# Five input-projection units beside the adaLN loads, and the residual gate summed in the last gate group

## The chip, the cores and the metric

The kernel runs on one core of a Trainium2 chip. The metric is the device time of one execution in microseconds (us), as the median of several runs. The core has TensorE (matmul; PE in the profile, with its weight loads as PEld), VectorE (DVE), ScalarE (ACT), GpSimd (POOL) and SyncE (SP), which here issues nearly all DMA transfers; each works through its own queue in order and waits on semaphores.

## What is computed

One layer of an encoder trunk, 256 tokens, width D = 2048, all in float32:

```python
mod = c @ ada_w + ada_b                       # one row of 6 x 2048
sh1, sc1, gt1, sh2, sc2, gt2 = split(mod, 6)
h = rmsnorm(x, norm1_g) * (1 + sc1) + sh1
u = h @ w_in                                  # A 512, B 2x512, C 3x512, D 512, gates 4x2048
y_a = pool_mixer(u_A); y_b = conformer_conv(u_B)   # B: a * sigmoid(gate), conv 31, LayerNorm, silu, @ w
y_c = (bg * conv3(cg * xv)) @ sc_w_out             # C
y_d = fft2(u_D).real @ fnet_w_out                  # D
merged = sum_k sigmoid(gate_k) * y_k
x = x + gt1 * (merged @ w_o)
h2 = rmsnorm(x, norm2_g) * (1 + sc2) + sh2
x = x + gt2 * hier_moe(h2, ...)               # 32 experts, top 1 group of 4, top 2 of 8
return rmsnorm(x, final_g)
```

## The kernel before

The four engine programs are written by hand, each a straight list of instructions with semaphores. `h` is held transposed (`hT`: 16 k tiles of 128 channels x 256 tokens). The ring has 7 slots of 2 MiB (128 x 4096 elements); slots 0 to 3 take weight blocks in turn, slot 4 (`BW`) the branch weights, slot 5 (`ADA`) adaLN tiles, slot 6 later `h_hi`.

**The head.** Shift and scale of the first modulation are vector-matrix products over 2 x 16 MiB of `ada_w`. VectorE makes them: for each k tile it multiplies the weight rows by `c` and adds them to `acc` (L1294, L1296); TensorE then sums over the partitions by products with a column of ones (`head_sums`, L541), VectorE adds the bias (L1304, L1306), and ScalarE modulates four k tiles (L1033). This is done in four parts of 512 columns, so that a quarter of `hT` is ready at a time. With each part TensorE takes the first `HEAD` = 3 of seven input units (512 columns of `w_in` each, `UNIT_COLS`: B gate, B value, C, C, C, D, A) over the four k tiles that are ready (L557), into six of the eight PSUM banks; the last two banks hold the sums. SP's order for a part is four ada blocks of 2 MiB (`load_head`, L350), then three weight blocks of 1 MiB (`load_head_w`, L359).

**The other units.** Units 3 and 4 (the third and first column blocks of C) run after the head over all 16 k tiles (`unit_T`, L571), then units 5 and 6 (`unit_N`, L584), with the two LayerNorm sums between them (L593, L600), then the DFT products (L612, L634, L635) and the pooling (L620). VectorE makes the convolution of 31 taps (L1332 to L1335) and that of 3 (L1353). GT1 (16 MiB of `ada_w`) is loaded in eight blocks (`load_gt1`, L384), summed by VectorE between its other steps (L1276, L1278), reduced by 32 one-column products (L640), and kept as a column.

**The gates.** Four groups of four units of 512 columns, each over 16 k tiles. Every weight is split in two float32r halves: ScalarE copies the high half (`gate_high`, L1095), VectorE subtracts for the low half (`gate_low`, L1403), `AHEAD` = 3 pieces of 128 x 1024 ahead, and TensorE makes three products for each (L658 to L660), eight pieces a unit. Behind each unit stand the branch's own products (`gate_y`, L628), with VectorE's merging (L1451, L1456). Beside groups 0 to 2 the adaLN vectors SH2, SC2 and GT2 are summed from tiles of 1 MiB (L1394) and reduced (`sum_ada`, L690). SP issues for each unit two gate blocks of 2 MiB (L363), behind each two adaLN tiles (L417), and behind every other unit's tiles a 2 MiB block of branch weights (L444). Group 3 has no adaLN tiles. GT1's row is made from its column there: VectorE spreads it on a diagonal (`diag`, L1478), TensorE multiplies by ones (`gate_row`, L709), ScalarE copies (L1121). Then come `w_o`, the router and the experts.

```python
def ada_tiles(g, k, n):
    vec = SH2 + g
    for i in range(n):
        sp.wait_ge(acc_step, ADA1 + 16 * g + k + i - 1)
        sp.dma_start(slot(ADA)[:, i % 2 * D:(i % 2 + 1) * D], ada_v[:, k + i, vec * D:(vec + 1) * D]
                     ).then_inc(ada_tile[i % 2], 16)
```

## Time and profile before

| | us |
|---|---|
| runs, not profiled | 1859.21, 1859.7, 1860.25 |
| median | 1859.7 |
| profiled execution, its own time | 1858.33 |
| its span, first to last instruction | 1856.5 |
| TensorE matmul busy | 1763.9 (95%) |
| VectorE busy | 899.4 (48%) |
| ScalarE busy | 393.7 (21%) |
| DMA | 641.92 MB, mean 346 GB/s |
| mean granted TensorE clock | 0.981 |

All times in the rows are from the start of the span. The slices cut the span in 40 equal parts of 46.4 us; a digit is the busy share in tenths. The chain of work that ended last is followed back from the last instruction, at each step to what released it. A matmul of float32 data is listed as two instructions.

### The profile page before, as it was taken

To read this page: it belongs to the slowest core of one execution; us is meant where nothing else is said; L and a number is where in the kernel's file an instruction comes from. 1 tells how busy PE (TensorE), PEld (TensorE's weight loads), DVE (VectorE), ACT (ScalarE), POOL (GpSimd) and SP (SyncE) were. 2 spreads that over 40 slices of the span, in tenths; PEclk is the share of its full clock that TensorE was granted. 3 is DMA by queue.
4 is the path that set the end of the run, shared out by engine and by line. 5 is a ranking of instruction groups with operands and counts; after the bars stand their busy time and mean duration, and the time that the engine had idled before them with its cause. 6 is when DMAs were issued, how large, how long until landed. Compare 5 with 4: busy or idle time off the path is not lost.

```text
span 1856.5 us, 26120 instructions
## 1 busy us (share of the span) xinstructions
PE 1763.9 (95%) x10306; PEld 1016.1 (55%) x10306; DVE 899.4 (48%) x1087; ACT 393.7 (21%) x477; POOL 0.9 (0%) x5
## 2 busy tenths in 40 slices
PE   1979999999999999999999999999999999999996
PEld 1868747786777677687444444444444443434342
DVE  5876766866757644457432333333233332323334
ACT  3010014432322333334211101111011111101011
POOL 0000000000000000000000000000000000000000
PEclk8989999989989999999999999999999999999998
DMA  9996597779868945355699999999999999999995
GB/s 374 386 387 257 191 378 291 295 274 351 303 249 317 339 151 212 148 189 237 247 422 422 422 422 422 422 422 422 423 421 422 422 422 422 422 423 421 422 422 237
DMA packets 137004, 641.92 MB, mean 346 GB/s; under 512 B 8578, under 2 KB 8706, under 8 KB 76674
## 3 DMA queue, kind: packets, MB, share of 16 engines
q1 hardware_dynamic: 136256, 637.08, 86.2%
q10 hardware_dynamic: 562, 2.55, 0.4%
q0 software_dynamic: 144, 1.70, 0.2%
q8 instruction: 30, 0.49, 0.1%
q14 instruction: 12, 0.10, 0.0%
HBM read 639.20 MB, written 2.10 MB: 345 GB/s over the span
## 4 chain that ended last, share of the span: by engine, by line
PE 68%; DMA 24%; DVE 6%; ACT 1%; issue 1%; SPq 0%; DVEq 0%; ACTq 0%
DMA ring<-in_exp_w 19%; PE ps L925 16%; PE ps L889 6%; PE ps L658 5%; PE ps L659 5%; PE ps L660 5%; PE ps L628 5%; DVE r_m L1296 4%; PE ps L912 3%; PE ps L867 3%; PE ps L571 3%; PE ps L584 3%; DMA ring<-in_branch_w 2%; DMA ring<-in_ada_w 2%; PE ps L753 2%; PE ps L754 2%
## 5 line engine op out<-in xcount | busy, mean ns | idle before, releaser
L925 PE MATMUL ps<-ring 128*64 128x512 f32 x2048 | 464.8, 596 | 5.8 <-DMA ring<-in_exp_w 5.8
L925 PEld LDWEIGHTS ps<-ring 128*64 128x64 f32 x2048 | 143.1, 137 | 291.7 <-issue 291.7
L1664 DVE TENSOR_TENSOR r_h<-r_h,ps 128x1024 f32<-128x1024 f32 x124 | 145.8, 1218 | 205.8 <-PE ps L912 205.8
L659 PE MATMUL ps<-g_lo,h_hi 128*128 128x512 f32 x512 | 201.7, 394 | 0.0
L1637 DVE TENSOR_TENSOR r_c<-ps,scale 128x512 f32<-128x512 f32 x65 | 44.7, 688 | 292.6 <-PE ps L867 291.7
L1209 ACT ACTIVATE r_m<-ps 128x512 f32<-128x512 f32 x32 | 19.1, 597 | 697.7 <-PE ps L925 697.7
L658 PE MATMUL ps<-mix_hi,h_hi 128*128 128x512 f32 x384 | 157.9, 411 | 0.0
L1095 ACT ACTIVATE mix_hi<-ring 128x1024 fp32r<-128x1024 f32 x96 | 101.7, 1062 | 261.1 <-PE ps L660 261.1
L1403 DVE TENSOR_TENSOR g_lo<-ring,mix_hi 128x1024 fp32r<-128x1024 f32 x96 | 117.5, 1225 | 77.7 <-ACT mix_hi L1095 76.9
L660 PE MATMUL ps<-mix_hi,h_lo 128*128 128x512 f32 x384 | 151.6, 395 | 0.0
L867 PEld LDWEIGHTS ps<-r_c,xparts 128*128 128x128 bf16 x3120 | 108.8, 118 | 50.9 <-issue 49.5
L912 PE MATMUL ps<-ring,r_m 64*128 64x512 f32 x496 | 123.2, 615 | 0.0
L867 PE MATMUL ps<-r_c,xparts 128*128 128x64 bf16 x3120 | 115.8, 198 | 1.3 <-ACT xparts L1164 1.3
L889 PE MATMUL ps<-r_b,r_c 128*64 128x512 f32 x496 | 113.3, 598 | 0.0
L889 PE MATMUL ps<-ring,r_c 128*64 128x512 f32 x496 | 111.7, 592 | 0.0
L659 PEld LDWEIGHTS ps<-g_lo,h_hi 128*128 128x128 f32 x512 | 97.7, 191 | 23.2 <-issue 3.1
L1394 DVE SCALAR_TENSOR_TENSOR r_m<-ring,col,r_m 128x2048 f32<-128x2048 f32 x45 | 105.5, 2345 | 0.0
L628 PE MATMUL ps<-ring,r_b 128*128 128x512 f32 x208 | 94.2, 604 | 10.3 <-DMA ring<-in_branch_w 6.0
L557 PE MATMUL ps<-r_h,ring 128*128 128x256 f32 x384 | 90.8, 401 | 5.0 <-ACT r_h L1033 5.0
L1296 DVE SCALAR_TENSOR_TENSOR r_m<-ring,col,r_m 128x512 f32<-128x512 f32 x120 | 90.2, 752 | 4.3
L557 PEld LDWEIGHTS ps<-r_h,ring 128*128 128x128 f32 x384 | 77.7, 203 | 16.9 <-issue 5.3
L912 PEld LDWEIGHTS ps<-ring,r_m 64*128 64x128 f32 x496 | 42.7, 186 | 79.5 <-issue 79.5
(267 smaller groups left out, 1745.8 us busy)
## 6 DMA issues: line engine op xcount, KB each, us to landing
ring<-in_exp_w SPq DMA_DIRECT2D x320, 1024.0 KB, 20.2
ring<-in_w_in SPq DMA_DIRECT2D x40, 2048.0 KB, 10.1
r_b<-in_exp_w SPq DMA_DIRECT2D x64, 1024.0 KB, 22.1
ring<-in_ada_w SPq DMA_DIRECT2D x24, 2048.0 KB, 18.7
ring<-in_ada_w SPq DMA_DIRECT2D x48, 1024.0 KB, 5.1
ring<-in_w_o SPq DMA_DIRECT2D x8, 2048.0 KB, 7.7
ring<-in_w_in SPq DMA_DIRECT2D x12, 1024.0 KB, 14.9
ring<-in_branch_w SPq DMA_DIRECT2D x6, 2048.0 KB, 9.7
```

Source lines behind the costliest of these rows:

```text
L557: last = mm(u[:, f, :], head_w(i)[:, kk, f * P:(f + 1) * P], hT[:, k, :], start=(k == 0 and f % 2 == 0), stop=(k == KT - 1), skip_group_ch ...
L628: last = mm(ps[:, y_bank(n) + t, :], lhs(k, t), rhs(k), start=(k == 0), stop=(k == kts - 1))
L658: mm(ps[:, b + t, :], h, hi[:, cols], start=(k == 0), stop=False)
L659: mm(ps[:, b + t, :], h, lo[:, cols], start=False, stop=False)
L660: last = mm(ps[:, b + t, :], h_lo[:, k, t * P:(t + 1) * P], hi[:, cols], start=False, stop=(k == KT - 1))
L867: last = mm(gat[:, kk, :], xparts_k[:, i, t, k // 4, k % 4, :], chosen[:, t, 0:NWIN], start=(t == 0 and i == 0), stop=(t == TT - 1 and i = ...
L889: last = mm(ps[side * NWIN:(side + 1) * NWIN, 4 + b, :], hid[:, f, :], chunk(CHUNKS + f)[:, q * MIX:(q + 1) * MIX], start=(f == 0), stop=( ...
L912: last = mm(ps[:, (6, 4)[b] + side, :], pair_wT[half, t * P:(t + 1) * P], y_sb[half, b, :], start=True, stop=True)
L925: last = mm(ps[m * NWIN:(m + 1) * NWIN, 2, :], xe[:, k, :], chunk(2 * c + m)[:, kk * F:(kk + 1) * F], start=(k == 0), stop=(k == KT - 1))
L1296: ins = V.scalar_tensor_tensor(out=total, in0=w, scalar=ccol[:, k:k + 1], in1=total, op0=ALU.mult, op1=ALU.add)
L1403: V.tensor_tensor(g_lo[:, q, (x % 4) * 1024:(x % 4 + 1) * 1024], slot(q)[:, (x % 4) * 1024:(x % 4 + 1) * 1024], g_hi[x % 4].bitcast(F32), ...
L1664: V.tensor_tensor(x1n, x1n, ps[:, (6, 4)[b]:(6, 4)[b] + 2, :].rearrange("p b n -> p (b n)"), ALU.add).then_inc(added, 1)
```

## The change

- The head carries five units. `HEAD` is 5; units 3 and 4 are made in each part over its four k tiles, one after the other into the same two banks that also hold the sums, and VectorE adds each quarter to a total in SBUF (`add_part`, `late`). `ORDER` is the order of the units in a part. `unit_T` is gone.
- The ada blocks hold four k tiles of both vectors, VectorE's step is 1024 elements wide and there are 64 of them rather than 128. Three blocks instead of four are in flight (slots 5, 6 and the room of `r_b`), the weights use slots 0 to 4.
- x is loaded by SP ahead of everything else, no longer by ScalarE's queue; `mix_consts` waits for the third part.
- GT1 leaves the middle. It is loaded in the last gate group in 32 half tiles of 512 KB (`gt1_tile`), issued by SP behind the group's gate blocks, and summed by VectorE behind each `gate_low` (`gt1_piece`) onto an accumulator that was zeroed and has the bias in its first partition. TensorE makes the row straight from it with a product of ones; `diag` and its column are gone. Two blocks of `w_o` are issued between the tiles.
- Unit 5 and half of unit 6 run ahead of the first LayerNorm sum. The root, the last LayerNorm product and Silu are moved behind the first three gate pieces; `h_hi` is made earlier.

The core of the diff (SP, then TensorE, ScalarE, VectorE):

```diff
-ADA_FIRST = 4
-HEAD = 3
+ADA_FIRST = 3
+HEAD = 5
+ORDER = [[3, 0, 4, 1, 2]] * 3 + [[3, 0, 1, 4, 2]]
...
+        def head_ada(i):
+            return (slot(5), slot(6), r_b[:, :])[i % ADA_FIRST].rearrange("p (k v n) -> p k v n", k=4, v=2)
+
+        def used(part, n):
+            return HEAD * part + ORDER[part].index(n) + 1
...
+            def load_head(part, piece):
+                i = 4 * part + piece
                 if i >= ADA_FIRST:
-                    sp.wait_ge(acc_step, 8 * (i - ADA_FIRST + 1))
...
+                    sp.wait_ge(acc_step, 4 * (i - ADA_FIRST + 1))
+                elif i == 2:
+                    sp.wait_ge(sq_done, 2)
+                for v in range(2):
+                    sp.dma_start(head_ada(i)[:, :, v, :],
+                                 ada_v[:, 4 * piece:4 * piece + 4, v * D + part * PART:v * D + (part + 1) * PART]
+                                 ).then_inc(ada_in[i % ADA_FIRST], 16)
...
-                if q == 3:
-                    sp.wait_ge(acc_step, 104)
-                elif q < 7:
-                    sp.wait_ge(head_used, (8, 10, 12)[q - 4])
-                else:
-                    sp.wait_ge(w_used, q - 6)
+                sp.wait_ge(head_used, (3 * HEAD, 3 * HEAD, used(3, 0), used(3, 2))[q - Q_UNIT])
...
+            sp.dma_start(x_in, x_v).then_inc(x_loaded, 16)
...
+            def gt1_tile(k, half):
+                if k:
+                    sp.wait_ge(acc_step, ADA2 + 2 * (k - 1) + half + 1)
+                else:
+                    sp.wait_ge(acc_step, ADA2)
+                sp.dma_start(slot(ADA)[:, 2048 + half * 1024:3072 + half * 1024],
+                             ada_v[:, k, GT1 * D + half * 1024:GT1 * D + (half + 1) * 1024]).then_inc(ada_tile[half], 16)
...
                         if g < N_BRANCH - 1:
                             ada_tiles(g, 4 * j + 2 * i, 2)
+                        else:
+                            if j == 0 and i == 0:
+                                sp.wait_ge(acc_zero, 1)
+                                sp.dma_start(acc[0:1, :], gt1_bias).then_inc(bias_in, 16)
+                            if j == 3:
+                                load_wo(i)
+                            for k in (4 * j + 2 * i, 4 * j + 2 * i + 1):
+                                for half in range(2):
+                                    gt1_tile(k, half)
...
+            pool.wait_ge(head_used, 3 * HEAD)
             pool.dma_start(r_c[:, :], mix_consts).then_inc(mixc_in, 16)
...
+                pe.wait_ge(acc_step, 16 * (part + 1))
+                if part:
+                    pe.wait_ge(part_added, 2 * part)
...
-                for n in range(HEAD):
+                for n in ORDER[part]:
...
+                    if n == 4:
+                        pe.wait_ge(part_added, 2 * part + 1)
+                    u = tiles((0, 4, 2, 6, 6)[n])
...
-                        if n == 0:
+                        if n == 3:
                             pe.wait_ge(h_ready, k + 1)
...
+            pe.wait_ge(sig_ready, 1)
+            unit_N(5, (0, 1))
+            pe.wait_ge(v_ready, 1)
+            unit_N(6, (0,))
             pe.wait_ge(conv_done, 1)
+            pe.wait_ge(part_added, 8)
...
+            unit_N(6, (1,))
...
-            pe.wait_ge(acc_step, ADA1)
-            for k in range(KT):
-                last = mm(ps[:, 6, k:k + 1], acc[:, k * P:(k + 1) * P], ones[:, 0:1], start=True, stop=True)
-            last.then_inc(summed, 1)
...
-                    last = mm(ps[:, 4 + m, :], ones, diag[:, o:o + 4, :], start=True, stop=True)
+                    n = 2 * half + m
+                    last = mm(ps[:, 4 + n, :], ones, acc[:, n * MIX:(n + 1) * MIX], start=True, stop=True)
...
-            pe.wait_ge(row_saved, 1)
+            pe.wait_ge(acc_step, ADA2 + 32)
+            pe.wait_ge(unit_saved, UNITS - 1)
+            gate_row(0)
+            pe.wait_ge(m_parts, 3)
             gate_row(1)
...
             for x in range(AHEAD):
                 gate_high(0, x)
+            act.wait_ge(inv_ready, 2)
+            A(mean, mean, ACT.Sqrt).then_inc(root_done, 1)
+            act.wait_ge(conv_done, 3)
+            for m in range(MT):
+                A(brT[:, 1, m, :], brT[:, 1, m, :], ACT.Silu, bias=col[:, C_LNB + m:C_LNB + m + 1],
+                  scale=col[:, C_LNG + m:C_LNG + m + 1]).then_inc(conf_ready, 1)
...
+            def add_part(part, n):
+                v.wait_ge(head_used, used(part, n))
+                total = late[:, n - 3, :]
+                products = ps[:, 6:8, :].rearrange("p b n -> p (b n)")
+                if part == 0:
+                    ins = V.tensor_copy(total, products)
+                else:
+                    ins = V.tensor_tensor(total, total, products, ALU.add)
+                ins.then_inc(part_added, 1)
+                v.wait_ge(part_added, 2 * part + n - 2)
+
+            for part in range(4):
+                total = head_acc(part)
+                for k in range(KT):
+                    i = 4 * part + k // 4
+                    if part and k in (0, 8):
+                        add_part(part - 1, 3 + k // 8)
+                    if k % 4 == 0:
+                        v.wait_ge(ada_in[i % ADA_FIRST], 32 * (i // ADA_FIRST + 1))
+                    w = head_ada(i)[:, k % 4, :, :]
...
+            add_part(3, 3)
+            v.wait_ge(head_used, used(3, 1))
+            v.wait_ge(sig_ready, 1)
...
+            v.wait_ge(root_done, 2)
+            V.tensor_tensor(brT[:, 1, :, :], brT[:, 1, :, :], mean.unsqueeze(1).broadcast_to([P, MT, S]),
+                            ALU.mult).then_inc(conv_done, 1)
...
+            def gt1_piece(k, half):
+                v.wait_ge(ada_tile[half], 3 * 128 + 16 * (k + 1))
+                v.wait_ge(bias_in, 16)
+                cols = acc[:, half * 1024:(half + 1) * 1024]
+                V.scalar_tensor_tensor(out=cols, in0=slot(ADA)[:, 2048 + half * 1024:3072 + half * 1024],
+                                       scalar=ccol[:, k:k + 1], in1=cols, op0=ALU.mult, op1=ALU.add
+                                       ).then_inc(acc_step, 1)
...
-                        if not last and i % 2 == 1:
+                        if last:
+                            gt1_piece(4 * j + i // 2, i % 2)
+                        elif i % 2 == 1:
                             ada_one(g, 4 * j + i // 2)
...
-            v.wait_ge(mod_ready, 8)
-            V.tensor_tensor(diag, ident.unsqueeze(1).broadcast_to([P, KT, P]),
-                            mod[:, GT1, :].unsqueeze(2).broadcast_to([P, KT, P]), ALU.mult).then_inc(diag_ready, 1)
+            v.wait_ge(mod_ready, 7)
+            V.memset(acc, 0.0).then_inc(acc_zero, 1)
```

## Rows read from the trace of the kernel before

**Rows 1.** Slices of the span: DMA share in tenths, GB/s.

```profile
DMA  9996597779868945355699999999999999999995
GB/s 374 386 387 257 191 378 291 295 274 351 303 249 317 339 151 212 148 189 237 247 422 422 422 422 422 422 422 422 423 421 422 422 422 422 422 423 421 422 422 237
```

**Rows 2.** Stretch: busy (x) per engine; last: TensorE clock, DMA, GB/s.

```profile
60.00:70.00 10.00, 10.00 (x48) 8.81 (x47) 9.54 (x14) 0.00 (x0) 0.00 (x0) 1.00 1.05 387
```

**Rows 3.** Timeline, head: start, us, engine, line, operation, count [idle before].

```profile
46.80 1.86 PE L541 MATMUL ps<-keep,r_m 128*128 128x1 f32 x8 [11.09 <-DVE r_m L1296]
...
49.97 22.85 PE L557 MATMUL ps<-r_h,ring 128*128 128x256 f32 x96 [1.31 <-ACT r_h L1033]
...
72.66 2.11 PE L541 MATMUL ps<-keep,r_m 128*128 128x1 f32 x16
...
76.03 20.96 PE L557 MATMUL ps<-r_h,ring 128*128 128x256 f32 x96 [1.25 <-ACT r_h L1033]
```

**Rows 4.** Groups, 0 to 320 us: xcount | busy us, mean ns | idle.

```profile
L1296 DVE SCALAR_TENSOR_TENSOR r_m<-ring,col,r_m 128x512 f32<-128x512 f32 x120 | 90.2, 752 | 4.3
...
L571 PE MATMUL ps<-r_h,ring 128*128 128x256 f32 x256 | 55.4, 379 | 0.0
...
L1278 DVE SCALAR_TENSOR_TENSOR r_m<-ring,col,r_m 128x2048 f32<-128x2048 f32 x15 | 35.3, 2352 | 15.5 <-DMA ring<-in_ada_w 15.2
...
L1324 DVE TENSOR_TENSOR r_m<-ps,r_m 128x1024 f32<-128x1024 f32 x1 | 1.2, 1228 | 17.8 <-PE ps L557 17.8
```

**Rows 5.** Chain of work that ended last: start us, us, what.

```profile
160.50 55.25 PE ps L571 x256
215.75 1.73 PE ps L593 x8
...
287.91 3.46 PE ps L640 x32
...
317.55 3.78 PE ps L628 x4
...
344.16 1.72 PE ps L628 x4
...
522.06 7.24 PE ps L690 x32
```

**Rows 6.** Timeline, ScalarE and VectorE ahead of the first gate.

```profile
253.80 2.07 ACT L1054 ACTIVATE r_b<-r_b,col 128x256 f32<-128x256 f32 x4
...
288.87 2.94 ACT L1095 ACTIVATE mix_hi<-ring 128x1024 fp32r<-128x1024 f32 x3
...
289.95 3.50 DVE L1403 TENSOR_TENSOR g_lo<-ring,mix_hi 128x1024 fp32r<-128x1024 f32 x3 [5.19 <-ACT mix_hi L1095]
```

**Rows 7.** Stretches around the pool product, columns as in rows 2.

```profile
313.00:317.50 4.50, 0.27 (x2) 0.00 (x0) 4.46 (x2) 1.97 (x2) 0.00 (x0) 0.90 1.03 369
317.50:321.50 4.00, 3.95 (x5) 1.85 (x6) 0.14 (x1) 0.00 (x0) 0.00 (x0) 0.50 0.99 400
```

**Rows 8.** Chain, group 1's second branch matrix.

```profile
473.75 2.27 DVE r_m L1394
...
476.41 9.80 DMA ring<-in_branch_w
486.25 7.13 PE ps L628 x16
```

**Rows 9.** Line 417, the adaLN tiles of 1 MiB: least, median and most.

```profile
DMA to landing us min/median/max: 4.8/5.1/13.8
```

**Rows 10.** DMA issues, 481 to 488 us: xcount, KB, us to landing.

```profile
ring<-in_ada_w SPq DMA_DIRECT2D x2, 1024.0 KB, 11.7
ring<-in_w_in SPq DMA_DIRECT2D x1, 2048.0 KB, 15.6
```

**Rows 11.** Chain around the last gate group's first unit.

```profile
649.65 3.47 PE ps L690 x32
...
675.04 6.87 PE ps L628 x16
```

More of the change, by code:

```diff
@@ L74, in build @@
 def build(nc, x, ada_w, w_in, pool_w, pool_scale, branch_w, w_o, router_w, exp_w1, exp_w3, exp_w2, final_g,
-          columns, router_b, keep_consts, mix_consts, iota_const, out):
+          columns, router_b, gt1_bias, keep_consts, mix_consts, iota_const, out):
     with ExitStack() as ctx:
@@ L204, in build @@
         ada_in = [sem(f"ada_in{i}") for i in range(ADA_FIRST)]
-        ada_more = [sem(f"ada_more{i}") for i in range(2)]
+        part_added = sem("part_added")
+        sig_ready = sem("sig_ready")
+        v_ready = sem("v_ready")
+        cx_ready = sem("cx_ready")
+        acc_zero = sem("acc_zero")
+        bias_in = sem("bias_in")
         ada_tile = [sem(f"ada_tile{i}") for i in range(2)]
@@ L357, in load_head_w @@
                 if part >= 2:
-                    sp.wait_ge(head_used, HEAD * (part - 2) + n + 1)
+                    sp.wait_ge(head_used, used(part - 2, n))
                 sp.dma_start(head_w(i), win_v[:, 4 * part:4 * part + 4, UNIT_COLS[n]:UNIT_COLS[n] + MIX]
@@ L445, in _ @@
                                      br_v[g - 1, :, :, j * MIX:(j + 2) * MIX]).then_inc(bw_in, 16)
-            for n in range(8):
+            for n in range(2, 8):
                 if n == 2:
@@ L547, in _, with unit_N @@
                 head_sums(part)
[L548 removed]
+                for n in ORDER[part]:
                     i = HEAD * (part % 2) + n
                     pe.wait_ge(head_w_in[i], 16 * (part // 2 + 1))
[L551 removed]
+                    if n == 4:
+                        pe.wait_ge(part_added, 2 * part + 1)
+                    u = tiles((0, 4, 2, 6, 6)[n])
                     for kk in range(4):
                         k = 4 * part + kk
[L554 removed]
+                        if n == 3:
                             pe.wait_ge(h_ready, k + 1)
                         for f in range(4):
+                            if n < 3:
+                                begin, end = k == 0, k == KT - 1
+                            else:
+                                begin, end = kk == 0, kk == 3
                             last = mm(u[:, f, :], head_w(i)[:, kk, f * P:(f + 1) * P], hT[:, k, :],
[L558 removed]
+                                      start=(begin and f % 2 == 0), stop=end, skip_group_check=True)
                     last.then_inc(head_used, 1)
[L561 to L577 removed]
+            def unit_N(n, halves):
+                for half in halves:
                     q = Q_UNIT + 2 * (n - HEAD) + half
@@ L1277, in ada_chunk @@
                     else:
[L1278 removed]
+                        ins = V.scalar_tensor_tensor(out=total, in0=w, scalar=ccol[:, k:k + 1], in1=total,
                                                      op0=ALU.mult, op1=ALU.add)
[L1280 to L1299 removed]
@@ L1300, in _ @@
+                    ins.then_inc(acc_step, 1)
+                    v.wait_ge(acc_step, 16 * part + k + 1)
                 ks = slice(4 * part, 4 * part + 4)
@@ L1340, in _ @@
             v.sem_inc(conv_done, 1)
-            v.wait_ge(w_used, 2)
-            v.wait_ge(unit_saved, 3)
-            step(V.tensor_tensor(cxpad[:, :, 1:1 + S], tiles(4), tmp[0].rearrange("p (c t) -> p c t", c=MT), ALU.mult))
-            v.sem_inc(unit_saved, 1)
-            z = tmp[0].rearrange("p (c t) -> p c t", c=MT)
+            add_part(3, 4)
+            v.wait_ge(head_used, used(3, 2))
+            step(V.tensor_tensor(cxpad[:, :, 1:1 + S], tiles(2), late[:, 0, :].rearrange("p (c t) -> p c t", c=MT), ALU.mult))
+            v.sem_inc(cx_ready, 1)
             c0 = steps[0]
@@ L1405, in gate_low @@
                                 ALU.subtract).then_inc(g_lo_done, 1)
-            v.wait_ge(h_split, 1)
-            v.wait_ge(w_used, 8)
-            for i in range(4):
+            v.wait_ge(w_used, 4)
+            for i in range(2, 4):
                 V.tensor_tensor(h_lo[:, 4 * i:4 * i + 4, :], hT[:, 4 * i:4 * i + 4, :],
```

210 lines of the change are left out of this document (58 added, 152 removed).

## The prediction

> **What bounds the kernel now.** I read the slices first, then the stages by stretches, then the chain of work in order of time. Up to some 140 us the transfer engines are full and TensorE is not: the slices show the share and the rate of the transfers, and the stretch shows 387 GB/s and the full TensorE clock side by side [rows 1, 2]. From 160 us on TensorE is busy all the time up to the experts, whose weights fill the transfer engines again from some 915 us to the end, at 422 GB/s [rows 1]. The chain says the same: VectorE's sums beside the loads, then TensorE from 160.50 on, units 3 and 4 in 55.25 us, unit 5, unit 6 and the mixers up to 291 [rows 5]. So whatever makes TensorE reach the experts earlier is worth its full length, and whatever makes it wait in between costs its full length. The change does one of each: it takes two units out of the TensorE-bound stretch and puts them beside the loads (a gain), and it puts 32 transfers of GT1 into the last gate group, ahead of that group's branch weights in SP's queue (a wait). The answer is the difference of the two.
>
> **The five units beside the loads.** A unit of 16 k tiles takes 55.4/2 = 27.7 us at the full clock (256 instructions, 216 ns from one to the next) [rows 4, 5], so a quarter of it takes 6.92 us, and three quarters 20.8 us, which is the 20.96 us measured once TensorE was warm [rows 3]. Five quarters are 34.6 us. Between two parts lie the sums, their read-out and ScalarE's first modulation: 72.8 to 76.03, that is 3.2 us, 3.3 taken [rows 3]. A part then costs TensorE 37.9 us.
> The transfers of a part grow from 11 to 13 MiB, 13.6 MB, 35.2 us at 387 GB/s [rows 2]. VectorE's 16 steps of 1024 elements have no row; 512 elements take 752 ns and 2048 take 2352 [rows 4], so 1.29 us each, 1.32 with the gap, 21.1 us a part, plus two adds of 1.23 us (the row of a product out of PSUM [rows 4]) and small steps: 24.5 us. But its second add waits for the third unit of the part before; from there 1.25 + 8 x 1.32 = 11.8 us are left, against 13.8 us of TensorE's last two units. So TensorE bounds the parts, by 2 us before VectorE and 2.7 before the transfers.
> The first part: x now goes first on SP's queue, then the pieces of 2 MiB at 5.4 us each. From about 2 us on at that rate, x and the small constants end at about 9, the pieces land at 14.9, 20.3, 25.7 and, since the fourth waits for the first to be used up, 31.1; four steps later it is 36.4. Before, the sums were ready at 46.8 and the units began at 49.97, 3.2 us on, with half of the sums done earlier [rows 3]; with both halves behind the last step I take 5.1. The units begin at 41.5. Then 34.6 + 2.2 (the cold start: 22.85 against 20.7 [rows 3]) + 3 x 37.9 gives 192.0 for the end of all five, where the old kernel ends units 3 and 4 at 215.75 [rows 5]. **Term 1: -23.8 us.** From both sides: if the first part starts only when it did, -15; if every gap were free, -34.
> The long convolution starts on VectorE when three units of the last part are there, at 178.2, and takes 50.5 as before: 229. TensorE asks for it only after unit 5 and half of unit 6, at 192 + 41.2 = 233. It stays hidden, with 4 us to spare. mix_consts and the four loads of units 5 and 6 go out from about 154 on and have more than 20 us.
>
> **Between the units and the gates.** Unit 5, unit 6, the two LayerNorm sums, the DFT and pooling are the same instructions. GT1's 32 one-column products (3.46 us [rows 5]) fall away, but the first gate piece still needs ScalarE's copy and VectorE's rest behind the last DFT copy, and these ended at 291.2 in the old kernel, just as the 3.46 us did [rows 5, 6]. So that removal is worth nothing: TensorE waits 3.3 us instead. Moved behind three gate copies are now the root, VectorE's product and four Silu steps, with two table loads, some 5.3 us on ScalarE (2.07 of it the Silu steps [rows 6], the rest the root, the hand-overs and the loads); TensorE has three pieces of 2.73 us in hand then. By my count piece 3 is ready 0.3 us late, and VectorE is 1.4 us behind at the end of the first gate unit, where TensorE already waited 4.3 us, to 317.55, for its product on the pool weights [rows 5, 7]. **Term 2: +1.7 us** (0 to 4).
>
> **The last gate group.** Here the order on SP's queue decides. For each four pieces it issues a 2 MiB gate block and two weight tiles; the 2 MiB of branch weights come after the eighth piece's tiles, for units 0 and 2 of a group. In groups 1 and 2 that is how it is already: the branch weights are issued at 476.41, right after VectorE's step at 473.75 to 476.02 released the last tile, they land 9.8 us later, and TensorE, which was ready at 485.0, starts at 486.25 [rows 8]. In group 3 the old kernel has no tiles, its branch weights go out early and TensorE never waits: 653.1 to 675.04 is the bare 21.9 us of a unit [rows 11].
> Now group 3 has half tiles, (k, half), and the issue of one waits for the step on the same half one k before. The last one ahead of the branch weights, (3,1), waits for the step on (2,1), which VectorE runs behind the rest of piece 5 of the unit. At best that is 5 x 2.73 + 1.07 + 1.24 + 1.32 = 17.3 us into the unit, against 12.8 for group 1. With 0.5 MiB ahead, the branch weights take 9.8 - 1.35 = 8.5 us: 26.5 at best, where TensorE needs them at 21.8 (22.7 in unit 2, after the turning of merged). So 4.7 and 3.8 us of waiting are the floor.
> I don't take the floor, because the half tiles themselves are late. One is issued only two pieces (5.4 us) before it is used. No row has one of 0.5 MiB; 1 MiB takes 4.8 to 5.1 us when nothing is ahead, and up to 13.8 when something is [rows 9], so 3.5 (estimate: 1.35 less) to 4.8. But before k = 2 and 3 (and 10 and 11) SP has put a gate block of 2 MiB, and the queue is served in order: a 1 MiB tile issued behind 2 MiB blocks took 11.7, and a block 15.6 [rows 10]. So (2,0), issued at 12.9, lands at 20.9 instead of 16.4. Stepping through unit 0 from TensorE's first gate product: the memset and its hand-over 2.0, the bias row and (0,0) land by 6.3, steps end at 7.6, 10.2, 12.9, 15.4, then the block holds up (2,0): 22.2, 24.8; branch weights issued at 25.6, landed at 34. TensorE needs them at 21.8: it waits 12.3 us. Unit 2 in the same way: it waits 8.9 us. At the 422 GB/s of the experts' slices [rows 1] it is 11.1 and 7.9. The middle of the two sums: **Term 3: +20.1 us** (8.5 to 23). The pieces in between stay ahead of TensorE, and GT1's last step ends 2 us before the last branch product does. The four products of the row take the same time as before, and the last copy of it is as exposed as it was.
>
> **The clock.** After 4.3 us of idling the granted clock fell to 0.50, and 4 products took 3.78 us instead of 1.72, the next unit 1 us more: 3.1 us in all [rows 5, 7]. Both waits of group 3 are longer than that. **Term 4: +6.3 us.** The shorter gaps are open. Of 3.2 us, filled half with one-column products, one passed at full clock (72.8 to 76.0 [rows 3]); such products alone, in sum_ada, once came with half the clock (7.24 us for 3.46 us of them [rows 5]) and once did not (3.47 [rows 11]). There are four such chances now, three between parts and the one ahead of the gates; I count one stretch of 3.2 us. **Term 5: +3.2 us** (0 to 13). The sums of groups 0 and 1 were both cold in the old kernel, some 6.5 us each with what follows them; that they come out otherwise can give back up to 13 us.
> The Trainium skill ("TensorE: Matmul & The Clock Gate", Part 1: The HAM clock gate) says that the throttled state is the default, and that the monitor runs freely, so that the same products meet it in different phases. That agrees with the two unlike sums above, and it is why I leave the sums' phases as they were and widen the range.
>
> **Sum.** -23.8 + 1.7 + 20.1 + 6.3 + 3.2 = +7.5 us. The profiled execution took 1858.3 us (span 1856.5 and 1.8 around it); that gives 1865.8, and for the median of the runs, 1859.7, 1867.2.
>
> **Rivals.** (1) Faster: the branch weights of group 3 aren't held up by the blocks, VectorE keeps pace, and the waits are the floor, 4.7 + 3.8. The first is then about as long as the one that dropped the clock, the second shorter: +3.1. -23.8 + 1.7 + 8.5 + 3.1 = -10.5, 1849; with one warm sum less, 1852. For it: the tiles are small and 16 engines serve them. Against it: every branch load of groups 1 and 2 took its 9.7 to 11 us in order. It decides from a total wait in group 3 below 12 us. A cold sum that turns warm helps to this side too. 0.2.
> (2) No change: the forecast with the waits right, and one cold sum phase gone (-6.5), 1861. 0.2.
> (3) The parts are longer than TensorE's work: VectorE's second add and the slots of three pieces make the loop. At 2 us of slack, a step of 1.5 us rather than 1.32 adds 1.2 us a part; steps of 1.6 (752 x 2 and the gap, the nearest row doubled) add 2.5 us in each of three parts and 4 in the first: +10, 1878. 0.12.
> (4) Every gap of 3.3 us halves the clock: four stretches instead of one, +9.6, 1877. The page named above speaks for it where it says that idling throttles; the row at 72.8 speaks against. 0.13.
> The forecast itself has 0.35.
>
> **How the numbers follow.** Eight in ten lie between 1850 and 1881: the floor of the waits at one end, rivals 3 and 4 with a little over at the other. A measurement of this kernel tells about 0.2%, 3.7 us, from no change. Faster by more: rival 1, 0.2. Within it: rival 2, 0.2. Slower by more: forecast and rivals 3 and 4, 0.6.
>
> **What would show it.** Term 1: units end near 192, each part 38 us apart, TensorE busy from 41 on. Term 2: the first gate product some 3.3 us after the last DFT product. Term 3: in the last group the branch weights are issued about 25 and 21 us into units 0 and 2, and TensorE waits for them 12 and 9 us, in two pieces. Term 4: a clock of 0.50 behind both. It would be wrong if the branch weights landed within 24 us of the unit's start, or if the head ended above 200 or below 185.

## The result and the profile after

The changed kernel took 1866.57 us (median of 12 runs, 1860.85 to 1874.83) beside 1859.01 us for the kernel before (12 runs, 1857.37 to 1861.1): a ratio of 1.0045, 95% interval 1.0031 to 1.0059. It is slower by 7.6 us, twice the 3.7 us (0.2%) that the prediction took as the least that can be told from no change; the forecast was 1867.2. The profiled execution has a span of 1864.2 us where the old one had 1856.5.

First the chain of work through the head and up to the gates (start us, us, what). L579 is the line of the five head units, L592 units 5 and 6, L1285 VectorE's steps, L636 the products of a branch.

```profile
1.74 13.40 DMA ring<-in_ada_w
...
15.95 1.30 DVE r_m L1285
...
41.74 36.55 PE ps L579 x160
...
81.22 34.77 PE ps L579 x160
...
156.61 36.46 PE ps L579 x160
193.07 41.20 PE ps L592 x96
...
295.14 3.78 PE ps L636 x4
```

Five units end at 193.07, where the old kernel ended units 3 and 4 at 215.75 [rows 5]; VectorE's step takes 1.30 us, and a part repeats every 37.7 us where no clock was lost. The product on the pool weights, L636 at 295.14, answers to 317.55 [rows 5]. TensorE waits twice on the way there, for the first gate piece and just ahead of that product, where the old kernel waited 4.28 us; its timeline (in brackets the idle time before, and what ended it):

```profile
268.54 0.50 PE L661 MATMUL ps<-mix_hi,h_hi 128*128 128x512 f32 x1 [3.32 <-DVE g_lo L1376]
...
295.14 3.78 PE L636 MATMUL ps<-ring,r_b 128*128 128x512 f32 x4 [4.50 <-DVE ring L1400]
```

Then the last gate group, in the same chain, from the reduction of GT2 (L692) to the first product on w_o (L751). Transfers from in_ada_w are GT1's half tiles; L711 is the product of ones that makes GT1's row.

```profile
625.20 3.48 PE ps L692 x32
...
641.99 8.39 DMA ring<-in_ada_w
...
654.53 8.98 DMA ring<-in_branch_w
663.56 8.63 PE ps L636 x16
...
725.48 9.16 DMA ring<-in_branch_w
734.68 8.90 PE ps L636 x16
...
766.25 6.87 PE ps L636 x16
773.12 3.45 PE ps L711 x8
...
777.66 0.50 PE ps L751
```

The branch weights of unit 0 were issued at 654.53, 25.9 us behind the first gate product, and landed at 663.51; in the old kernel the same products followed theirs without a gap [rows 11]. The waits of this stretch, 625 to 780 us (us in all, times, longest):

```profile
DVE r_m L1413 <- DMA ring<-in_ada_w: 24.9, 15, 5.1
...
PE ps L636 <- DMA ring<-in_branch_w: 21.7, 2, 11.4
```

SyncE's timeline shows why they were late: the issue of the branch weights (L462) stands behind four half tiles (L423), and each of those waits for a step of VectorE. An entry that lasts 12 us is the queue standing at such waits; ahead of unit 2's branch weights, issued at 725.48, it stands for 13.35 us.

```profile
641.99 12.51 SPq L423 DMA_DIRECT2D ring<-in_ada_w  x4
654.53 0.43 SPq L462 DMA_DIRECT2D ring<-in_branch_w  x1
```

Of line 423, the half tiles, the time to landing was, answering to rows 9 and 10 of before:

```profile
DMA to landing us min/median/max: 3.6/4.5/13.3
```

And the stretches (columns as in rows 2): after, the whole last group and its two waits; before, the same group.

```profile
629.00:778.00 149.00, 126.23 (x482) 90.40 (x480) 94.21 (x76) 41.45 (x40) 0.00 (x0) 0.92 0.73 267
...
656.00:667.00 11.00, 3.44 (x5) 1.65 (x6) 3.37 (x3) 0.00 (x0) 0.00 (x0) 0.53 1.01 393
728.00:739.00 11.00, 4.32 (x6) 1.90 (x7) 3.53 (x3) 0.00 (x0) 0.00 (x0) 0.53 1.02 415
```

```profile
653.00:775.00 122.00, 120.93 (x482) 88.10 (x481) 54.81 (x45) 41.43 (x40) 0.00 (x0) 1.00 0.46 168
```

The account by places, as starts of the same work:

| | before | after | difference |
|---|---|---|---|
| the head's last unit ends (before: units 3 and 4) | 215.75 | 193.07 | -22.7 |
| product on the pool weights | 317.55 | 295.14 | -22.4 |
| first product of the last group | 653.1 | 628.7 | -24.4 |
| first product on w_o | 775.05 | 777.66 | +2.6 |
| end of the span | 1856.5 | 1864.2 | +7.7 |

Everything that the head gave (24.4 us) went in one group of gates, which grew by 27.0 us. Another 5.1 us came behind it, of which two stretches at half the clock in the w_o stage, 786 to 790 and 861 to 865, are some 3.4 us (1.7 each, the time lost by a clock of 0.57 over 4 us); where the other 1.7 went wasn't looked into.

### The profile page after: what moved, and what is told of

It is laid out like the page before. It is cut to its first block, busy times and chain, and to the rows that moved or that the text cites. A ratio compares the mean times of both kernels' runs of the same rounds, so it can differ in the third digit from the quotient of the medians.

```text
span 1864.2 us, 26124 instructions
## 1 busy us (share of the span) xinstructions
PE 1766.5 (95%) x10273; PEld 1013.6 (54%) x10274; DVE 899.9 (48%) x1046; ACT 392.7 (21%) x476; POOL 0.8 (0%) x5
## 4 chain that ended last, share of the span: by engine, by line
PE 70%; DMA 22%; DVE 4%; ACT 1%; issue 1%; SPq 0%; DVEq 0%; ACTq 0%
PE ps L923 18%; DMA ring<-in_exp_w 15%; PE ps L579 8%; PE ps L887 8%; PE ps L636 5%; DMA ring<-in_ada_w 4%; PE ps L910 4%; PE ps L865 4%; PE ps L661 4%; PE ps L663 4%; PE ps L662 4%; DMA ring<-in_branch_w 3%; PE ps L592 3%; PE ps L751 2%; PE ps L753 2%; PE ps L752 2%
## 5 line engine op out<-in xcount | busy, mean ns | idle before, releaser
L579 PE MATMUL ps<-r_h,ring 128*128 128x256 f32 x640 | 142.6, 386 | 5.0 <-ACT r_h L1030 5.0
L579 PEld LDWEIGHTS ps<-r_h,ring 128*128 128x128 f32 x640 | 123.7, 194 | 22.6 <-issue 5.3
L636 PE MATMUL ps<-ring,r_b 128*128 128x512 f32 x208 | 97.6, 622 | 30.8 <-DMA ring<-in_branch_w 26.3
L661 PEld LDWEIGHTS ps<-mix_hi,h_hi 128*128 128x128 f32 x384 | 74.1, 193 | 21.9 <-DVE g_lo L1376 3.7
## 6 DMA issues: line engine op xcount, KB each, us to landing
ring<-in_exp_w SPq DMA_DIRECT2D x320, 1024.0 KB, 19.7
```

Of the source, the lines that this page charges most:

```text
L579: last = mm(u[:, f, :], head_w(i)[:, kk, f * P:(f + 1) * P], hT[:, k, :], start=(begin and f % 2 == 0), stop=end, skip_group_check=True)
L636: last = mm(ps[:, y_bank(n) + t, :], lhs(k, t), rhs(k), start=(k == 0), stop=(k == kts - 1))
L661: mm(ps[:, b + t, :], h, hi[:, cols], start=(k == 0), stop=False)
```

## The experiments

Each kernel is the changed one with the edit shown. Ratios are to the kernel before, on the same chip.

**The changed kernel again.** 

> The changed kernel as it is, profiled and timed once more, as the measure for the other kernels and for its spread. In the profile shown of it the last gate group took 148.9 us from the end of the third sum (628.7) to the first product with w_o (777.7), against 121.9 before, and TensorE waited 11.4 and 10.3 us in it for branch weights. Queue theory (the waits are made by the order on SP's queue): the same two waits within 0.5 us. Clock theory for the spread of 14 us between its runs: the waits repeat and the stretches with a clock of 0.50 lie elsewhere or are of other length. Rival (transfers differ from run to run): the waits themselves differ by some us. Time 1866, between 1860 and 1874.

1866.66 us (5 runs, 1863.02 to 1871.5) beside 1860.22; ratio 1.0042 (1.0029 to 1.0054). The two waits in its last group are 22.3 us, the longer 11.7: they repeat, with the order of the queue.

**The branch weights ahead of the tiles.**

`branch_w` holds the wait and the transfer of L462.

```diff
+    if j == 0 and i == 0:
+        branch_w(g, 0)
     for k in (4 * j + 2 * i, 4 * j + 2 * i + 1):
         for half in range(2):
             gt1_tile(k, half)
+    if j == 2 and i == 0:
+        branch_w(g, 2)
```

> Only SP's order in the last gate group changes: the branch weights of unit 0 are issued ahead of all half tiles, those of unit 2 behind the first four tiles of that unit. The same transfers, the same VectorE steps. Queue theory: both waits (21.7 us) go, and with them most of the 10.2 us lost to a clock of 0.50 in that group; the group takes 122 to 125 us, the kernel 24 to 27 us less than the changed one, some 1841. Rival (the group is longer because 16 MiB of tiles and 32 VectorE steps load it): the group stays above 140 us, the kernel gains under 8 us, 1859 or more.

1846.96 us (6 runs, 1845.98 to 1851.27), ratio 0.9936 (0.9923 to 0.9948): 19.7 us less than the changed kernel on the same chip, and faster than the kernel before. TensorE no longer waits for branch weights. But the group still takes 135 us, not the 122 to 125 that were expected, nor the 140 and more of the rival, and the kernel lies 6 us above the 1841 that were expected. Its chain now runs through the tiles alone (L1420 is L1413 here, L718 is L711):

```profile
639.83 9.51 DMA ring<-in_ada_w
649.36 1.30 DVE r_m L1420
650.67 3.83 DMA ring<-in_ada_w
...
753.66 1.30 DVE r_m L1420
755.00 5.41 PE ps L718 x8
```

Transfer, step, transfer, step, to the end of the group: each transfer waits for the step that frees its place, and no long wait of TensorE covers this loop any more. A half tile takes some 3.8 us when nothing is ahead and 8.3 to 9.5 when a block of 2 MiB is. VectorE waits 36.0 us for them in this group, so its gate pieces come late, and the row's product (L718) comes 2.9 us late behind VectorE's last step:

```profile
PE ps L668 <- DVE g_lo L1383: 6.0, 3, 3.4
```

So there were two mechanisms in the last group, and the prediction had only the first.

**GT1 taken out.** This kernel leaves out GT1's tiles and VectorE's sum of them; the row is the bias alone.

```diff
-    for k in (4 * j + 2 * i, 4 * j + 2 * i + 1):
-        for half in range(2):
-            gt1_tile(k, half)
...
-    if last:
-        gt1_piece(4 * j + i // 2, i % 2)
```

> Leaves GT1's sum out: no half tiles are loaded and no steps on them are made, the row is the bias alone; the branch weights keep their place in SP's program. It shows what GT1 costs in the last group in any order. Queue theory: as e1 within 3 us, since with a better order GT1 is hidden: group 121 to 123 us, kernel 1839. Rival (tiles and steps load the group by themselves): this kernel is 10 us or more faster than e1.

1833.19 us (4 runs, 1832.26 to 1833.84), ratio 0.9857 (0.9842 to 0.9871). The last group is bare TensorE work: 122.11 us of 123.

```profile
626.00:749.00 123.00, 122.11 (x480) 88.91 (x479) 54.05 (x44) 41.26 (x40) 0.00 (x0) 0.99 0.51 188
```

This is the floor for any way of loading GT1 there. The order of the queue is worth 19.7 us of the distance to it, and 13.8 us were still missing: more than the 3 us expected, and what the rival had asked for (10 us or more). Which of tiles, steps and latency makes them is not told by this run. Also, its runs lay 1.6 us apart, those of the changed kernel 8.5 to 14.

**A gate block out from between the tiles.**

```diff
-    if x < 8 or g < N_BRANCH - 1:
+    if g < N_BRANCH - 1:
         gate_w(g, x)
+    elif i == 0 and x < 8:
+        gate_w(g, x)
+        gate_w(g, x + 1)
```

> In the last group the second 2 MiB gate block of each unit is issued ahead of the unit's first tiles, no longer between tiles of k 1 and k 2 (and 9 and 10). The branch weights stay behind eight half tiles. The forecast split the waits in two: a floor of 4.7 and 3.8 us (the chain of steps that releases the last tile) and the rest from tiles held up behind that block. If that is right: branch weights issued some 21 and 18 us into units 0 and 2, waits of 6 to 8 and 4 to 6 us, sum 10 to 14 instead of 21.7, kernel 8 to 14 us less, 1852 to 1858. Rival (tiles are slow on their own, by their size or by VectorE): the waits stay within 3 us of 21.7 in sum.

1859.24 us (10 runs, 1854.38 to 1862.37), ratio 0.9996 (0.9987 to 1.0005): no difference to the kernel before, 7.4 us less than the changed one. In the chain the branch weights go out 22 us into the unit instead of 26 (L639 is L636 here, L1416 is L1413):

```profile
646.47 1.29 DVE r_m L1416
...
648.15 9.24 DMA ring<-in_branch_w
```

The waits of the group:

```profile
PE ps L639 <- DMA ring<-in_branch_w: 16.0, 2, 8.3
```

The waits fall from 22.3 to 16.0 us, where 10 to 14 had been expected and 19 or more by the rival. A part of them is the held-up tiles, as Term 3 had it; the larger part stays, and in the chain the last tile ahead of the branch weights still waits for a step of VectorE (646.47).

**The tiles on GpSimd's queue.** GT1's bias row goes there too, and the tiles have semaphores of their own.

```diff
 def gt1_tile(k, half):
     if k:
-        sp.wait_ge(acc_step, ADA2 + 2 * (k - 1) + half + 1)
+        pool.wait_ge(acc_step, ADA2 + 2 * (k - 1) + half + 1)
...
-    sp.dma_start(slot(ADA)[:, 2048 + half * 1024:3072 + half * 1024],
+    pool.dma_start(slot(ADA)[:, 2048 + half * 1024:3072 + half * 1024],
```

> The half tiles of GT1 are issued by GpSimd, which is idle, with the same waits; SP's program in the last group is that of the kernel before, with no wait for a tile in it. In e1 the chain of work in that group ran through the tiles alone: a load of 3.7 us or, behind a 2 MiB block, 8.3 to 9.5 us, then a step of 1.30 us, sixteen times over, and the group took 139 us from the end of its sum to the copy of the row. Loop theory (the tile loop is bound by its own latency, and the blocks ahead in the same queue make it too long): with a queue of its own a tile takes some 4 to 5 us throughout, 16 x 6 = 96 us, hidden; branch weights go out early; the group takes 119 to 123 us and the kernel comes within 4 us of e2, 1834 to 1838. Rival (the tiles' bytes or VectorE's 32 steps are the load): the group stays over 130 us, the kernel over 1843.

1854.74 us (12 runs, 1848.96 to 1861.73), ratio 0.9975 (0.9962 to 0.9988), 17 to 21 us above what was expected and within what the rival had asked for (over 1843; the tiles' bytes or VectorE's steps as the load). The run with both edits, below, has the same bytes and steps and none of this loss. TensorE waits for no branch weights here, and yet the group takes 137.7 us: the tiles no longer stand behind the blocks in SP's queue, but they are in flight beside them. The median to landing was 4.8 us by the page of the profile (4.5 for those of SP in the changed kernel), single ones took far longer, and the loop is the same. The chain of work, then the waits of VectorE and TensorE over the group:

```profile
703.68 10.09 DMA ring<-in_ada_w
```

```profile
DVE r_m L1413 <- DMA ring<-in_ada_w: 33.8, 19, 6.0
...
PE ps L661 <- DVE g_lo L1376: 9.6, 3, 4.8
```

Here the second queue took away the order and left the latency. Whether a tile issued by GpSimd is a little slower by itself was not tested.

The Trainium skill ("DMA: Bandwidth & Descriptors", Issuing engines are not separate DMA queues) says that transfers issued by SyncE, ScalarE and GpSimd run on the same 16 DMA engines. The trace agrees as far as it goes: VectorE's wait in this group is 33.8 us with GpSimd's queue and 36.0 with SyncE's (branch weights first in both).

**Four places for the half tiles.** The first half of `r_b` (branches 0 and 1) is not read in the last group; each place has a semaphore of its own.

```diff
+gt1_slot = [r_b[:, 0:2048], ring[:, 5, 2048:4096]]
 def gt1_tile(k, half):
-    if k:
-        sp.wait_ge(acc_step, ADA2 + 2 * (k - 1) + half + 1)
+    if k > 1:
+        sp.wait_ge(acc_step, ADA2 + 2 * (k - 2) + half + 1)
...
-    sp.dma_start(slot(ADA)[:, 2048 + half * 1024:3072 + half * 1024],
+    sp.dma_start(gt1_slot[k % 2][:, half * 1024:(half + 1) * 1024],
```

> The changed kernel, in which GT1's half tiles have four places rather than two: those of even k go to two thirds of the branch tiles' buffer that the last group no longer reads, those of odd k stay where they were. The issue of one then waits for the step two k before, not one. Order on SP's queue unchanged. Theory (the lead of the tiles sets both the tile loop and the late branch weights): the last tile ahead of the first branch weights waits for the step on (1,1), which ends about 12.8 us into the unit, not some 20; branch weights issued some 13 to 15 us in, landed at 22 to 25, waits 0 to 3 us each, 4 in sum (changed kernel 21.7), DVE waits for tiles under 10 us (24.9), the last group 124 to 128 us (148.9), kernel 1842 to 1848. Rival (the gate blocks of 2 MiB in the same queue set the pace, whatever the lead): waits for the branch weights stay above 12, the group above 137, kernel above 1853.

1845.98 us (5 runs, 1842.07 to 1850.53) beside 1859.14; ratio 0.9921 (0.9907 to 0.9935). With the order untouched, the longer lead alone takes away more than the change had cost (chain, then waits of the group; L638 is L636, L1415 is L1413):

```profile
649.55 12.36 DMA ring<-in_branch_w
```

```profile
PE ps L638 <- DMA ring<-in_branch_w: 6.1, 2, 4.8
DVE r_m L1415 <- DMA r_b<-in_ada_w: 5.9, 2, 3.4
```

The branch weights go out 16 us into the unit (633.6 to 649.55; 13 to 15 expected) and take 12.4 us with more in front of them, so the waits are 6.1 us rather than 4, and the group takes 131.6 us rather than 124 to 128. The total is within what was expected (1842 to 1848).

**Both: branch weights first, four places.** The edits of those two runs together.

> The run with the branch weights ahead of the tiles, and four places for the half tiles as well. Theory (what that run kept over the one without GT1, 13.8 us, is only the latency of a tile in a loop of two places): DVE's wait for tiles falls from 36 to under 10 us, no branch wait, the last group 123 to 126 us instead of 135, kernel 1833 to 1838, and a narrower spread than the changed kernel's 14 us. Rival (it is VectorE's own work of 32 steps of 1.30 us in the last group that costs the rest, or the transfers' share): no better than 1844.

1834.29 us (4 runs, 1833.64 to 1836.32), ratio 0.9865 (0.985 to 0.988). The last group is at the floor of the kernel without GT1, with the sum in it:

```profile
626.80:750.30 123.50, 122.39 (x481) 89.16 (x481) 92.74 (x77) 41.48 (x40) 0.00 (x0) 0.99 0.85 318
```

So what kept the last group at 135 us was latency in a loop of two places, and neither VectorE's 32 steps nor the transfers' share: VectorE has 92.7 us of work in 123.5, and the transfer engines are at 0.85. Of the 13.8 us, 11.6 came back (both against the kernel before on the same chip); the other 2.2 are not in this group.

**The start of the gates.** The run before, and on ScalarE the last DFT copy behind the first three `gate_high`, the root right behind the sums; on VectorE the product on `brT` ahead of the first `gate_low`.

```diff
-A(r_b[:, 3072:4096], ps[:, 2:4, :], ACT.Copy).then_inc(dft_saved, 1)
 for x in range(AHEAD):
     gate_high(0, x)
+A(r_b[:, 3072:4096], ps[:, 2:4, :], ACT.Copy).then_inc(dft_saved, 1)
```

> The run before, with the edits at the start of the gates: ScalarE's last DFT copy behind the first three gate copies, the root right behind the sums, VectorE's product on brT ahead of the first gate pieces' rests. Theory (TensorE's waits of 3.3 us for the first gate piece and some 2 for the pool product are exposed): 4 to 6 us less than the run before, 1828 to 1833. Rival (clock: one cold stretch more or less swallows it): within 2 us of the run before.

1832.38 us (4 runs, 1829.64 to 1835.19), ratio 0.9858 (0.9843 to 0.9873). In the profile the edit does what it should. First the run before, then this one, chain (L670 the first product of a gate, L645 the product on the pool weights):

```profile
267.30 0.50 PE ps L670
...
295.25 3.31 PE ps L645 x4
```

```profile
263.33 0.36 PE ps L670
...
289.55 3.78 PE ps L645 x4
```

The last DFT products end at 264.01 in the former and at 263.33 in the latter: the wait of 3.3 us is gone, and the product on the pool weights comes 5.7 us earlier, 5.0 without the head's own 0.66. But the medians differ by 1.9 us only, where 4 to 6 were expected and under 2 by the rival, and the two intervals overlap; that the edit pays its 5 us was not shown. The same edits on the tiles in GpSimd's queue:

> e10 and, ahead of the gates, the first three gate copies on ScalarE before the last DFT copy, the root and VectorE's product before the pool copy (the Silu steps behind the gate copies). Expected by the profile shown of the changed kernel, where TensorE waited 3.3 us (265.2 to 268.5) for the first gate piece and the product on the pool weights began at 295.1: the wait of 3.3 us goes, piece 3 is no longer late, the pool product begins 4 to 5 us earlier; the kernel 4 to 5 us less than e10. Rival (the time goes into the wait for VectorE ahead of the pool product): first gate product earlier, pool product not, no gain.

1852.02 us (6 runs, 1849.97 to 1857.22), ratio 0.9962 (0.9947 to 0.9977), 2.7 us below the kernel without them; in its profiled head the clock fell behind all three gaps. From the end of the head to the product on the pool weights the profiles show 98.4 us with the edits and 103.4 without, in both pairs, and yet twice the median moved by about half of that or less; what swallows the rest wasn't settled.

**The branch weights ahead of the tiles in groups 1 and 2 too.** In those groups TensorE waits 4.6 us for branch weights, in four waits of at most 1.2.

```diff
+    if g > 0 and j % 2 == 0 and i == 0:
+        branch_w(g, j)
     ada_tiles(g, 4 * j + 2 * i, 2)
```

> The run before, with the branch weights ahead of the adaLN tiles in groups 1 and 2 too (there TensorE waits 4.7 us for them in four waits of 1.2 or so). Theory: these waits go and the adaLN tiles behind them, with two places and a lead of four pieces, are still in time: 3 to 5 us less, 1825 to 1830. Rival: the tiles come late, VectorE's steps fall behind and the sums wait for them: 0 to 10 us more than the run before.

1831.8 us (5 runs, 1827.62 to 1834.02), ratio 0.9841 (0.9828 to 0.9855): not told apart from the run with the start of the gates, and above what was expected (1825 to 1830). The wait changed its owner (waits, 380 to 622 us):

```profile
DVE r_m L1376 <- DMA ring<-in_ada_w: 15.0, 4, 6.6
...
PE ps L670 <- DVE g_lo L1385: 2.3, 2, 1.8
```

These groups have two places for their tiles, and in the chain a tile behind the branch weights takes 11.3 us in the one and 10.0 in the other; TensorE then waits 2.3 us for VectorE instead, and behind the longer of these waits it lost another 1.7 us to a clock of 0.72 and 0.85 (452 to 460). It is the lesson of the last group on a smaller scale.

**x in ScalarE's queue, as before the change.**

```diff
-sp.dma_start(x_in, x_v).then_inc(x_loaded, 16)
+act.dma_start(x_in, x_v).then_inc(x_loaded, 16)    # behind keep, columns, router_b
```

> The changed kernel with x loaded by ScalarE's queue behind the constants, as in the kernel before. The forecast gave the earlier start of the first part (49.97 to 41.7 us) two causes without parting them: wider VectorE steps on smaller pieces, and x going first. Here x shares with the first two ada blocks, lands at some 13 to 15 us instead of 9.7, and the third block, which waits for both squares, is issued some 4 us later. If x going first matters: units begin 3 to 5 us later, all times behind shift by as much, kernel 1870 to 1872. Rival (the blocks are bound by the rate of transfers anyway): below 1 us.

1868.76 us (5 runs, 1864.82 to 1874.11), ratio 1.0040 (1.0022 to 1.0058). x lands at 13.6 us, and the units begin 1.7 us later than 41.74, where 3 to 5 were expected and under 1 by the rival:

```profile
2.24 11.35 DMA r_m<-in_x
...
43.47 6.68 PE ps L578 x16
```

**A dose of VectorE work.** One extra step behind the second add of the third part, three in the fourth part.

```diff
+    if k == 8:
+        for _ in range((0, 0, 1, 3)[part]):
+            step(V.tensor_tensor(r_m[:, 3072:4096], late[:, 0, :], late[:, 1, :], ALU.add))
```

> The changed kernel with extra VectorE steps of 1024 elements (1.23 us and a hand-over of 0.15 each, results not used) behind the second add of a part: none in the part loop's second pass, one in the third, three in the fourth. The forecast says that TensorE bounds the parts, with VectorE 2 us behind. In the profile shown of the changed kernel VectorE ended its steps 1.9 us ahead of TensorE's units in each part (76.4 and 78.3; 114.1 and 116.0; 151.8 and 153.7). TensorE-bound: the units begin at 81.2, 118.9 (+0), and 156.6 + 4.2 - 1.9 = 158.9 for the last part, so the one extra step costs nothing and the three cost 2.3 us. Rival (VectorE's loop is the bound): the one step costs 1.4 us, the three 4.2.

One run, 1874.88 us, with the clock down behind every gap of the head; what counts is the profile. TensorE's timeline (idle time before in brackets):

```profile
118.08 1.84 PE L557 MATMUL ps<-keep,r_m 128*128 128x1 f32 x16
...
159.54 3.14 PE L557 MATMUL ps<-keep,r_m 128*128 128x1 f32 x16 [1.91 <-DVE r_m L1288]
```

One step costs nothing: the sums at 118.08 follow the units without a wait. Three take VectorE from 145.18 to 148.96, 3.8 us, and make the sums wait 1.91 (2.3 expected): VectorE has 1.9 us to spare in a part, where the prediction said 2.

## Why the prediction was right, and where it was not

The sum came out: +7.5 us forecast, +7.7 in the profiled span and +7.6 in the medians. With runs of the changed kernel 14 us apart, agreement to 0.2 us is luck; what counts is each term, and the first four missed by +1.1, -1.4, +1.6 and -1.0 us, which nearly cancel.

**Term 1** (-23.8) was -22.7. The units began at 41.74 (forecast 41.5) and ended at 193.07 (192.0). Parts are 37.7 us without a loss and up to 39.5 with one. The walk from x through 13.4 us of the first block and 16 steps of 1.30 held, and so did the statement that TensorE bounds a part, by 2 us before VectorE: the dose showed 1.9. Rival 3 falls with it. The place of x ahead of the blocks, which the term held implicitly, is worth 1.7 us.

**Term 2** (+1.7) came to +0.3 (from -22.7 to -22.4). The wait for the first gate piece is 3.32 us as forecast, and the removed one-column products gave nothing, as forecast. The 0.3 and 1.4 us foreseen behind it came to 0.2: TensorE waited 4.50 us ahead of the product on the pool weights, for 4.28 before.

**Term 3** (+20.1) measured 21.7 and, in another execution, 22.3. The step from the queue's order to the time of issue, 25.6 us into the unit, was 25.9; landed at 34.8 for 34; the wait of unit 0 was 11.4 for 12.3, that of unit 2 10.3 for 8.9. The half tiles took 3.6 us at least and 4.5 in the median, inside the 3.5 to 4.8 that the prediction had to bound without a row, and 8.4 behind a block, 8.0 forecast (12.9 to 20.9). Rival 1, the floor of 8.5 us, needed tiles that no block holds up; with a block moved out of the way the waits still were 16.0.

**Term 4** (+6.3) is what the group grew by beyond the waits: 27.0 - 21.7 = 5.3. Both waits dropped the clock (0.53 in each stretch), and the branch products behind them took 8.63 and 8.90 us for 6.87, which is 3.8 us; the other 1.5 is a low clock at the group's first products (628.7 to 632.1), behind the sum, where the prediction had none. So a wait cost some 1.9 us of clock rather than 3.1.

**Term 5** (+3.2, 0 to 13) was named for gaps between the parts and came there in part only: one stretch of 1.7 us at 158. Some 3.4 us came in the w_o stage instead, where the prediction had none, and of the 2.0 us by which the lead grew up to the last group (22.4 to 24.4), 1.7 came because the clock behind the sums of group 1 took 3.4 us for 5.1 before. The size was about right and the place was not. Rival 4, a drop behind every gap, is what other executions of the same head did (below).

**Its sums.** Three don't come out as written. The floor of the waits: 17.3 + 8.5 is 25.8, not 26.5; 0.7 us between the step and the issue is not named (the trace has 0.4, from 654.15 to 654.53). Term 4: twice 3.1 is 6.2. Rival 3: only the 8 steps behind the second add count against the 2 us to spare, so steps of 1.5 us would have cost a part nothing and steps of 1.6 us 0.2 to 0.4; with the 4 us of the first part that is some +5, not +10. The first stands in the walk of Term 3 too (24.8 to 25.6) and made each wait 0.4 us too long there; the second adds 0.1 to the forecast; the third leaves it as it is.

**What the prediction did not see** lies in a sentence within Term 3: "The pieces in between stay ahead of TensorE, and GT1's last step ends 2 us before the last branch product does." In the changed kernel it came true: the last step ends at 770.93, 2.2 us before the last branch product (773.12).

```profile
769.64 1.29 DVE L1413 SCALAR_TENSOR_TENSOR r_m<-ring,col,r_m 128x1024 f32<-128x1024 f32 x1
```

But it is so only because TensorE itself stands still for 21.7 us. Once the branch waits were gone, the loop of tile and step held the group at 135 us, where TensorE's work is 123. The prediction walked through the loop up to the branch weights of units 0 and 2, to find their times of issue, and took the rest for granted. A walk to its end would have shown it, by an estimate from the changed kernel's chain: eight times 8.4 + 1.3 + 3.8 + 1.3 us, from 2.8 us into the group on, is 121 us, where TensorE's own work up to the row is 119 (the run with both edits). For the time of this change it made no difference, since the two overlap; for what to do about it, it made all of it. Against the kernel before on the same chip the changed one stood at +6.4 us, the reordered queue at -13.3, the lead of four places at -13.2, and the two together at -24.9: so each edit alone gave 19.6 to 19.7 us, and both 31.3. The last is about the gain of 24.4 us that the change had ahead of its last group, with nothing lost in that group.

## What to carry to other kernels

A transfer whose issue waits for a consumer's step makes everything behind it in its queue wait for that consumer too: put what the critical engine needs next ahead of it, not behind it (19.7 us here). And for each such loop compare its lead (places x the time between two steps) with the latency under load, not the free one: here two places gave 5.5 us (2 x 2.73) against 8.4, four places 10.9. A wait that is found and removed may have hidden a second one, so run the kernel with the whole of the suspected work taken out, to learn how far the floor is.

## What the runs showed of the hardware

**The same instructions lose the clock in one execution and not in another.** The first 200 us of the four kernels with four places are the same program, and that of the changed kernel too. The head's last unit ended at 193.07 in the changed kernel, and at 191.17, 191.83, 196.95 and 198.18 in the four others; by the trace most of the difference is the granted clock: behind none, one or all of the three gaps of 2.9 us between the parts it fell to 0.50, and a part that began so took 1.4 to 3.0 us longer. Two parts in the chain of the run with four places alone, the latest, and then of the one with the start of the gates, the earliest:

```profile
81.90 37.76 PE ps L581 x160
...
161.72 36.46 PE ps L581 x160
```

```profile
81.01 34.77 PE ps L588 x160
...
156.40 34.77 PE ps L588 x160
```

A difference of 7 us in the head alone is of the size of the spread between the runs of one kernel, 5 to 14 us for most of these. The Trainium skill ("TensorE: Matmul & The Clock Gate", Part 1: The HAM clock gate) says that the clock's monitor runs freely, whenever the kernel starts; the trace agrees with it, in that 160 products of the same kind took 34.77, 36.21, 36.46 and 37.76 us. Two kernels without waits in the last group spread by 1.6 and 2.7 us over four runs, two others by 5.5 and 6.4 over four and five; what decides it stays open.

**A transfer's latency under load.** 0.5 MiB landed in 3.6 to 4.3 us alone, in 8.2 to 9.5 with 2 MiB issued just ahead in the same queue (13.3 at most in the changed kernel), and in up to 10.1 from another queue while blocks were in flight.
